# Decay rows of a recurrence step: a 32 KB landing spread by a VectorE shuffle, in place of a 1 MB broadcast transfer

## What is computed

```python
Acs = jnp.cumsum((dt * A).reshape(b, c, Q, G, R), axis=2)
seg = jnp.exp(jnp.where(tril, Acs[:, :, :, None] - Acs[:, :, None, :], -jnp.inf))
CB = jnp.einsum('bclgn,bcsgn->bclsg', Cc, Bc)
y_diag = jnp.einsum('bclsgr,bcsgrp->bclgrp', CB[..., None] * seg, xg)
```

## Time and profile before

| | |
|---|---|
| time, median of 3 runs | 4048.46 us |
| span of the profiled execution (its own time) | 5878.7 us |
| TensorE busy, share of the span | 5726.4 us, 97% |
| VectorE busy | 2887.4 us, 49% |
| ScalarE busy | 1648.5 us, 28% |
| POOL busy | 1285.3 us, 22% |
| bytes moved by DMA | 1444.45 MB |
| mean granted TensorE clock in the profile | 0.555 |

### The profile page before, as it was taken

One profiled execution on the slowest core, in us unless ns is written; L12 is line 12 of the kernel. 1 busy time (PEld: TensorE's weight loads), 2 busy tenths in 40 slices (PEclk: granted clock), 3 DMA queues, 4 the chain that ended last, 5 costly groups with the idle time before them and its releaser, 6 DMA issues.

```text
span 5878.7 us, 40315 instructions
## 1 busy us (share of the span) xinstructions
PE 5726.4 (97%) x13374; PEld 2787.7 (47%) x13374; DVE 2887.4 (49%) x5745; ACT 1648.5 (28%) x4216; POOL 1285.3 (22%) x1094
## 2 busy tenths in 40 slices
PE   9999999999999998999999999899999999899999
PEld 5555555444444545444445545344445555222222
DVE  3321003665555455756555555756555554744443
ACT  3431101344422211244432211245422211222222
POOL 0000000222222221322222221322222221334343
PEclk6555555555555555555555555555555555555555
DMA  4222222767777775767777775777777775899997
GB/s 155 93 102 81 73 90 95 267 238 266 261 275 268 274 280 202 285 245 280 273 272 297 283 291 190 280 256 271 271 268 308 281 290 191 315 350 342 345 342 281
DMA packets 212948, 1444.45 MB, mean 246 GB/s; under 512 B 27256, under 2 KB 27256, under 8 KB 46340
## 3 DMA queue, kind: packets, MB, share of 16 engines
q0 software_dynamic: 164976, 1133.94, 52.0%
q1 hardware_dynamic: 47632, 307.80, 14.4%
q10 hardware_dynamic: 132, 0.12, 0.0%
HBM read 1439.31 MB, written 7.13 MB: 246 GB/s over the span
## 4 chain that ended last, share of the span: by engine, by line
PE 96%; DVE 2%; ACT 1%; issue 1%; DMA 0%; SPq 0%; ACTq 0%; DVEq 0%
PE banks L609 52%; PE sums L871 21%; PE banks L871 7%; PE banks L748 5%; PE banks L827 3%; PE banks L669 2%; PE banks L736 1%; PE banks L786 1%; PE banks L778 1%; PE banks L694 1%; PE banks L844 1%; DVE x L1479 1%; DVE rows L1470 0%; PE banks L637 0%; PE banks L700 0%
## 5 line engine op out<-in xcount | busy, mean ns | idle before, releaser
L609 PE MATMUL banks<-hT,ring 128*128 128x256 f32 x6656 | 2608.4, 583 | 4.7 <-DVE arena L1316 3.9
L609 PEld LDWEIGHTS banks<-hT,ring 128*128 128x128 f32 x6656 | 1507.5, 228 | 1151.7 <-issue 734.0
L576 POOL DMA_INDIRECT rows<-in_w_uv,idx x1024 | 1237.6, 1209 | 3600.3 <-PE sums L871 1981.3
L1470 DVE CUSTOM_DVE_ANT_0 rows<-rows,xn 128x1024 f32<-128x1024 f32 x1024 | 1241.6, 1220 | 530.8 <-DMA rows<-in_w_uv,idx 528.0
L871 PE MATMUL sums<-rows,diag 128*128 128x512 f32 x1612 | 1285.2, 970 | 70.0 <-ACT diag L1076 47.9
L1479 DVE SCALAR_TENSOR_TENSOR x<-rows,wgt,x 128x1024 f32<-128x1024 f32 x493 | 632.0, 1282 | 234.8 <-ACT wgt L1068 234.0
L871 PEld LDWEIGHTS sums<-rows,diag 128*128 128x128 f32 x1612 | 369.2, 232 | 791.7 <-issue 683.2
L1281 DVE SCALAR_TENSOR_TENSOR arena<-banks,pr,arena 128x254 f32<-128x254 f32 (+1 forms) x512 | 246.8, 482 | 354.6 <-ACT arena L965 340.9
L1063 ACT ACTIVATE gelu<-hid 128x2 f32<-128x2 f32 x512 | 102.9, 201 | 1100.7 <-DVE hid L1470 1099.3
L609 PE MATMUL banks<-yT,ring 128*128 128x256 f32 x1024 | 400.2, 582 | 0.0
L871 PE MATMUL banks<-rows,diag 128*128 128x512 f32 x512 | 393.7, 966 | 0.0
(11 more groups left out here) (205 smaller groups left out, 2955.8 us busy)
## 6 DMA issues: line engine op xcount, KB each, us to landing
ring<-in_w_ssd SPq DMA_DIRECT2D x96, 1024.0 KB, 5.4
ring<-in_w_att SPq DMA_DIRECT2D x64, 1024.0 KB, 6.1
ring<-in_w_mrg SPq DMA_DIRECT2D x52, 1024.0 KB, 8.4
arena<-a_rows POOLq DMA_DIRECT2D x32, 1024.0 KB, 7.6
ring<-in_w_qry SPq DMA_DIRECT2D x32, 1024.0 KB, 4.8
arena<-bias_tiles POOLq DMA_DIRECT2D x16, 1152.0 KB, 7.3
ring<-in_w_out SPq DMA_DIRECT2D x16, 1024.0 KB, 7.0
rows<-in_w_uv,idx POOLq DMA_INDIRECT x1024, 6.8
```

The costliest lines, as they stand in the source:

```text
L576: nc.gpsimd.indirect_dma_start(out=rows[n % NB][:, :], out_offset=None, in_=w_uv, in_offset=bass.IndirectOffsetOnAxis(ap=idx[:, t, s:s + 1 ...
L609: mm = pe.matmul(out, w[:, k * P:(k + 1) * P], rhs[:, k0 + k, :], start=start and k == 0, stop=stop and k == n - 1)
L1470: v.tensor_tensor_reduce(u, u, xn2[:, (n // SLOTS_T) % 3, :], 1.0, 0.0, ALU.mult, ALU.add, hid[:, k:k + 1]).then_inc(u_done, 1)
```

## The change

The transfer lands in partitions 0, 32, 64 and 96 only: 4 x 8 KB. VectorE then runs one stream shuffle over the whole buffer, in place, which copies within each block of 32 partitions the first partition to the other 31. The DMA gets its own semaphore `dr_in`, and `bc_in` now counts shuffles: VectorE waits for its own shuffle before it adds the masks, and POOL's write of `a_rows` in the next mixer waits on it.

```diff
+        aBC_rows = aBC.rearrange("p d h t -> p (d h t)")
...
-        aT_out, bc_in = count("aT_out", 16), count("bc_in", 16 * GROUPS)
+        aT_out, dr_in, bc_in = count("aT_out", 16), count("dr_in", 16 * GROUPS), count("bc_in", GROUPS)
...
                 def decay_rows(g):
-                    src = spread(a_dram[:, g * RH:(g + 1) * RH, :].rearrange("d h t -> d (h t)"), 0, P)
-                    pool.dma_start(aBC.rearrange("p d h t -> p d (h t)"), src).then_inc(bc_in.sem, 16)
+                    src = spread(a_dram[:, g * RH:(g + 1) * RH, :].rearrange("d h t -> d (h t)"), 0, P // 32)
+                    pool.dma_start(aBC[0:P:32].rearrange("p d h t -> p d (h t)"), src).then_inc(dr_in.sem, 16)
...
                 def mask(g):
-                    v.wait_ge(bc_in.sem, bc_in.at(m, 16 * (g + 1)))
+                    v.wait_ge(dr_in.sem, dr_in.at(m, 16 * (g + 1)))
+                    v.stream_shuffle(aBC_rows, aBC_rows, [0] * 32).then_inc(bc_in.sem, 1)
+                    v.wait_ge(bc_in.sem, bc_in.at(m, g + 1))
```

## The result

The changed kernel takes 4067.13 us (median of 4 runs, 4066.55 to 4072.21) against 4049.49 before: a ratio of 1.0047, 95% interval 1.0033 to 1.0061. It is 18 us slower. The forecast was 4027 us, a small gain; rival 2 gave 4072.

A forecast was written before the change was run, and what follows sets the result against it. It took transfers as nearest their limit, VectorE and TensorE close behind. Three later mixers at -5 - 2.6 us each give -23, the first mixer +2: -21 from 4048, so 4027 us, range 3985 to 4085.

The forecast's parts named there:

- rival 2: Ssd groups: VectorE becomes the bound, waits not caused by transfers stay; +24 us, 4072 us; chance 0.28.
- What the timed runs look like: Whole kernel at a higher clock than profiled: first part 622 us, middle 2697, tail 730; third mixer's groups 2 to 7 250.
- The shuffle's price: VectorE, 32 added shuffles of 128x2048: 2.4 us each, 77 us in all, 58 in the middle.
- the one-input row: Profile row, 637 ns for 128x768 of a one-input operation: lower bound of 1.7 us per shuffle, 54 in all.
- The transfer's worth: Decay transfers, 1.016 MB less each: 2.63 us at 386 GB/s, 63 us for 24 if transfers alone set the end.
- The overlap: Groups 2 to 7 of later mixers: transfers fall to 237 us, VectorE rises to 241.8; 245 taken, -5 us each.
- Its deciding point: Groups 2 to 7: VectorE binds once more than 8 us are idle for another reason than a gather.
- The first mixer: First mixer's groups: TensorE covers the shuffle, 2 us charged; 19 us without the cover.
- The first group of a mixer: Masks' wait for the transfer: 4 to 5 us instead of 7, some 3 back for 2.4 of shuffle, about nothing.
- Rival 4: POOL's queue: its wait for later exponents delays gathers; up to +58 us, 4106 at worst; chance 0.03.
- Rival 3: From the second mixer on transfers bind everywhere, shuffles fit in gather waits: -63 us, 3985 us; chance 0.12.

The follow-up runs named there:

- the early shuffle: Changed kernel with the shuffle of groups 1 to 7 moved ahead of the group's last ticks: 4070.36 us, ratio 1.0045.
- the two shuffles: Kernel before with its 1 MB transfer kept and two shuffles per group added, the second over the first's result: 4159.74 us, ratio 1.0274.
- the relief by TensorE: 62 instead of 50 of 100 expert sums of groups 2 to 7 on TensorE: changed kernel 4057.88 us, kernel before 4045.77 us.

## Why the prediction was wrong

Point by point:

- **What the timed runs look like: right for the stage, in part by luck.** From the profile at a clock of 0.55 I estimated 250 us for groups 2 to 7 of the third mixer; it is 247.7. The split that gave it was less good: the instructions that start at 1096 and 5040 us in that profile start at about 691 and 3362 us at the timed clock. So the first part takes 691 us where I had 622, and the tail 684 where I had 730. TensorE does not bind over the whole: it is busy 85%. Window 3 of the third mixer, where it is busy 34.0 of 34.5 us, is an exception that I did not see.
- **The shuffle's price: near.** 2.4 us expected, 2.51 measured; 80 us in all instead of 77. The 1.7 us of the one-input row is not borne out. The one-element-per-cycle rule of the Trainium skill, "VectorE: DVE Perf Modes", section "The perf-mode tier table", with its about 2400 ns, agrees with the 2506 ns measured to within 5%.
- **The transfer's worth: one step that failed.** "They move 366 x 267 = 97.7 MB, at 386 GB/s 253 us", against a stage of 250: I took the mean rate of the middle for the limit of each group. Transfers reach 427 GB/s in this program. Only windows 0 and 4 came near that, at 421 and 425, the others ran at 357 to 412, and only windows 0, 4 and 5 got shorter with less to move. The transfer alone was worth 16.7 us of the 63 that this rate gives, and 3.9 us of the 13 that the sum allows for the stage.
- **The overlap: the step that gave the wrong sign.** "VectorE stops it at 242. I take 245, -5 us" leaves VectorE 3 us of idle time in six groups, and gives no reason why its waits for other engines should end. Measured, the shuffles and what moved with them added 15.7 us of work, the idle time took up 10.0 of it, 14.7 us stay idle with no wait for a gather among them, and the stage is 253.4. That is rival 2, whose "if 16 us stay, a stage takes 258, +8" named the mechanism, with +24 us for the total where +18 was measured. It was also close for the stage: 16 us idle and +8 against 14.7 and +5.7. Its deciding point, 8 us of idle for another reason than a gather, had been passed before the change: of the 21.1 us of listed waits 16.6 were for ScalarE.
- **The first mixer: right.** TensorE covers the shuffle: groups 2 to 7 take 147.7 us before, after, and with the shuffle beside the 1 MB transfer.
- **The first group of a mixer: the sign is right, the size too large.** Window 0 of the later mixers got 0.4, 0.9 and 0.6 us shorter; the sum had 2.6 us for the first two groups. The landing went from 7.5 us (issue 59.5, masks 66.9) to 3.0 (63.1 to 66.1) in the first mixer. VectorE's waits for the decay rows in all mixers together went from 33.7 to 27.0 us, most of it the first one, of 20.8 and 25.2: in it POOL itself waits 13.5 and 13.7 us for its write of `a_rows` to land before it may read the rows back.
- **Rival 4 (POOL and the exponents): nothing of it.** POOL's wait in those six groups is 7.3 us after against 6.6 before.
- **Rival 3 (memory binds everywhere): wrong.** Five slices of about 100 us in a row run at 427 GB/s. So the 358 GB/s of the Trainium skill, "DMA: Bandwidth & Descriptors", section "Specifications", is not the limit that this core met.

That VectorE's time in the later mixers is what costs is shown by the windows, where the shuffle costs the same with either transfer, and by the early shuffle; the two shuffles and the relief by TensorE point the same way. Open is what sets the 14.7 us that VectorE keeps. 10.9 are listed as waits for ScalarE, the rest is in gaps too short to be listed, some 0.6 us in each window. No run took ScalarE's work away, so why the waits in window 6 gave back nothing is not shown. That moving 8.8 us of sums off VectorE gave only 3.2 us has one cause in the trace: windows 3 and 4 are then full on TensorE. Whether that is all of it no run shows.

## What to carry to other kernels

A mean rate over a stage hides which stretch is full: take windows as short as the loop body, and price a traded resource in each of them. Idle time of an in-order engine is not room for new work, and its share of a stretch doesn't tell: here the same shuffle cost 0.2 us in one window and 2.6 in another, with VectorE idle for nearly the same time. Look wait by wait whether new work would shorten it, and if that can't be told, price it in full. When a profile ran at another clock than the timed runs, its chain of waits answers a different question. Get one at the timed clock before trading one engine's time for another's.

## What the runs showed of the hardware

- The profiled execution of before ran for nearly all of its 5878.7 us at a granted clock of 0.55; every other profiled execution here, the same kernel's among them, was at 0.94 to 0.95. VectorE's rows are alike in both (1219 ns for L1295 at the lower clock, 1222 for the same line after), and TensorE's busy time is 5726 against 3427 us.
- In slices of about 100 us transfers reach 427 GB/s and no more: 427 in five slices in a row after, with gathers nearly alone, and up to 426 where weight loads run beside them.
- A stream shuffle of 128x2048 fp32 words in place takes 2.51 us, 10% more than the 2273 ns that the slope of `TENSOR_TENSOR` (692 and 1219 ns for 512 and 1024 columns) gives. The mask load before it shows as 14 ns.
- A transfer of 32 KB issued among gathers of 1 MB lands in 5.4 to 10.5 us (24 of them, after); with hardly a gather in the queue in 2.2 to 3.0 us (8 of them).
